# A two-layer decoder trunk on one core: the edges between its stages, its token lists and the order of its attention units

## The reference

```python
def rmsnorm(x, g):
    y = x * lax.rsqrt(jnp.mean(x * x, axis=-1, keepdims=True) + NORM_EPS)
    return y * g

def reference(...):
    h = x
    for layer in range(DEPTH):                       # DEPTH = 2
        xn = rmsnorm(h, norm_mix_g[layer])
        h = h + (rwkv7_time_mix(xn, ...) if layer == 0 else dilated_attention(xn, k_sh, v_sh, w_q, w_o))
        h = h + hier_moe(rmsnorm(h, norm_ffn_g[layer]), ...)
        if layer == 0:
            kv = rmsnorm(h, kv_norm_g) @ w_kv        # keys and values of all three groups
    return rmsnorm(h, final_norm_g)

def dilated_attention(xn, k_sh, v_sh, w_q, w_o):
    q = (xn @ w_q)                                   # 3 groups x 8 heads x 64
    # each group: windowed softmax attention with dilation 1, 4 or 16; also its log denominator
    alpha = softmax(stack(lses), axis=0)             # the groups are weighed by it and added
    return (sum(alpha * outs)) @ w_o

def hier_moe(x, ...):                                # 4 groups x 4 experts, top 1 group, top 2 inside
    for e in range(16):
        y = y + gate[:, e] * ((silu(t @ w_gate[e]) * (t @ w_up[e])) @ w_down[e])
```

## Time and profile before

| | us |
|---|---|
| median of 3 runs | 1559.42 (1558.93 to 1560.63) |
| the profiled execution, its own time | 1562.04 |
| its span, first to last instruction | 1560.3 |
| time mixer (to the first instruction of `moe` in layer 0) | about 521 |
| prologue of the experts, layer 0, to the first expert's product | 521 to 557 |
| experts of layer 0, to the second output of the last | 557 to 848 |
| attention stage | 867 to 1202 |
| experts of layer 1, with prologue | 1203 to 1548 |
| final norm | 1549 to 1560 |

### The profile page before, as it was taken

The page is one execution under the profiler, slowest core; times in us unless marked ns, Lnnn a source line. Parts: engine busy times, 40 slices in busy tenths (PEclk is TensorE's granted clock), DMA queues, the critical chain, the costliest instruction groups (busy, mean ns, idle before and its releaser), DMA issues. The chain is left out here.

```text
span 1560.3 us, 29684 instructions
## 1 busy us (share of the span) xinstructions
PE 1380.5 (88%) x11619; PEld 1077.1 (69%) x11619; DVE 1020.5 (65%) x1346; ACT 846.2 (54%) x1257; POOL 377.5 (24%) x413
## 2 busy tenths in 40 slices
PE   4999996776779899999998599999988899999993
PEld 2276686666664578788786487778767778787872
DVE  5627652445634488999996535675434698998986
ACT  6535552444421358888883334444542488888872
POOL 1112063435450013222223200001120023222322
PEclk9999897999999899999999699999978799999997
DMA  5042300052442579999995332121201799999974
GB/s 170 16 147 81 135 1 15 11 158 86 131 152 101 216 264 383 379 377 378 384 381 192 108 97 82 55 81 55 81 1 46 278 352 386 382 380 379 379 276 163
DMA packets 172042, 301.90 MB, mean 193 GB/s; under 512 B 34573, under 2 KB 44941, under 8 KB 171936
## 3 DMA queue, kind: packets, MB, share of 16 engines
q1 hardware_dynamic: 159648, 271.59, 49.0%
q0 software_dynamic: 11232, 24.61, 4.4%
q10 hardware_dynamic: 1056, 4.19, 0.7%
HBM read 279.96 MB, written 34.60 MB: 202 GB/s over the span
## 5 line engine op out<-in xcount | busy, mean ns | idle before, releaser
L1444 DVE TENSOR_TENSOR moe_wlo<-moe_raw,moe_whi 128x2048 fp32r<-128x2048 f32 x162 | 370.2, 2288 | 35.1 <-ACT moe_whi L1440 30.7
L1440 ACT ACTIVATE moe_whi<-moe_raw 128x2048 fp32r<-128x2048 f32 x192 | 367.0, 1916 | 24.0 <-PE all_bank L1453 22.7
L1451 PE MATMUL all_bank<-moe_whi,moe_xhi 128*128 128x512 f32 x512 | 207.0, 404 | 4.5 <-DVE moe_xlo L1500 4.5
L1452 PE MATMUL all_bank<-moe_wlo,moe_xhi 128*128 128x512 f32 x512 | 199.8, 390 | 0.0
L1453 PE MATMUL all_bank<-moe_whi,moe_xlo 128*128 128x512 f32 x512 | 199.7, 390 | 0.0
L1451 PEld LDWEIGHTS all_bank<-moe_whi,moe_xhi 128*128 128x128 f32 x512 | 96.0, 187 | 27.4 <-DVE moe_xlo L1500 4.4
L1453 PEld LDWEIGHTS all_bank<-moe_whi,moe_xlo 128*128 128x128 f32 x512 | 96.1, 188 | 21.0
L1613 POOL COPY moe_idxcol<-moe_idx 128x1 int32 (+1 forms) x30 | 34.4, 1145 | 312.9 <-PE all_bank L1463 312.9
L1452 PEld LDWEIGHTS all_bank<-moe_wlo,moe_xhi 128*128 128x128 f32 x512 | 96.2, 188 | 18.0
L1451 PE MATMUL all_bank<-moe_whi,moe_hhi 128*128 128x512 f32 x256 | 101.5, 397 | 3.0 <-issue 2.6
L1452 PE MATMUL all_bank<-moe_wlo,moe_hhi 128*128 128x512 f32 x256 | 100.6, 393 | 0.0
(11 more groups left out here) (436 smaller groups left out, 3024.3 us busy)
## 6 DMA issues: line engine op xcount, KB each, us to landing
moe_raw<-in_moe_w_gate_dram SPq DMA_DIRECT2D x64, 1024.0 KB, 9.4
moe_raw<-in_moe_w_up_dram SPq DMA_DIRECT2D x64, 1024.0 KB, 8.8
moe_raw<-in_moe_w_down_dram SPq DMA_DIRECT2D x64, 1024.0 KB, 8.3
attn_xhat<-in_w_kv_dram SPq DMA_DIRECT2D x10, 1024.0 KB, 5.1
out_dram<-all_gain SPq DMA_DIRECT2D x16, 512.0 KB, 4.0
attn_xhat<-in_attn_w_q_dram SPq DMA_DIRECT2D x6, 1024.0 KB, 5.0
all_h<-in_rwkv_w_k_dram SPq DMA_DIRECT2D x4, 1024.0 KB, 8.4
all_h<-in_rwkv_w_v_dram SPq DMA_DIRECT2D x4, 1024.0 KB, 5.0
```

The lines of the kernel that those rows point to most:

```text
L1440: nc.scalar.activation(whi[slot % SPLITS][:, :], raw[slot % 6][:, :], ACT.Copy).then_inc(m["hi_ok"], 1)
L1444: nc.vector.tensor_tensor(wlo[slot % SPLITS][:, :], raw[slot % 6][:, :], whi[slot % SPLITS][:, :].bitcast(fp32), ALU.subtract).then_inc(m[ ...
L1451: nc.tensor.matmul(bank[b][:, :], hi[:, k0 + k, :], wh[:, k, :], start=begin and k == 0, stop=False)
L1452: nc.tensor.matmul(bank[b][:, :], hi[:, k0 + k, :], wl[:, k, :], start=False, stop=False)
```

## The change

The kernel after does five things. (1) `final_norm` goes, and the experts' stage of layer 1 does its work: ScalarE takes the root of a tile right after its squares, VectorE normalises the tiles after the last addition, SyncE sends them out. Both `moe` and `attention` issue one square root on a constant before the squares of h. (2) The attention's first piece comes in two transfers, its split is made two rows of tiles at a time between those of the activations, and TensorE waits for each part of both instead of for all. (3) The token list is made of fp32r products; as an fp32r operand holds fewer bits, the number goes in two parts, 128 j less 512 and the row in the tile, in 32 columns, and VectorE adds the halves. `hot` lies in a weight buffer. (4) `combine` works tile by tile, and the last expert's additions of tile j - 1 follow those of tile j. (5) `beside` begins attention units at two of three steps up to step 35 and again from step 37 on.

```diff
@@ constants
-    for name, n, step, base, per_partition in (("down4", 4, -1, 4, 0), ("base16", 16, P, 0, 0), ("tokless", J, P, -T, 1)):
+    for name, n, step, base, per_partition in (("down4", 4, -1, 4, 0), ("base16", 16, P, 0, 0), ("tokrow", J, P, -T, 0), ("tokpart", 1, 0, 0, 1)):
@@ moe(nc, io, g, layer, result=None)
-        mtok = s.sb("mtok", [P, 2, J, NE])
+        mtok = s.sb("mtok", [P, 2, J, 2 * NE], fp32r)
...
-        hot = yo[:, :].rearrange("p (k j r) -> p k j r", k=2, j=J)
-        late = xn[:, :, :].rearrange("p a b -> p (a b)").rearrange("p (b k j r) -> p b k j r", b=4, k=2, j=J)
+        hot_in = lambda w: w[:, 0:2 * J * P].rearrange("p (k j r) -> p k j r", k=2, j=J)
+        hot, late = hot_in(wlo[3]), [None] + [hot_in(wlo[b]) for b in range(J - 1)]
...
+            if result is not None:
+                for j in range(J):
+                    sp.wait_ge(out_done, j + 1)
+                    sp.dma_start(result[0, P * j:P * j + P, :], h[:, j, :]).then_inc(stored, 16)
+                sp.wait_ge(stored, 16 * J)
...
             for k in range(2):
-                nc.gpsimd.tensor_tensor(mtok[:, k, :, :], ..., g["tokless"]..., ALU.mult).then_inc(mtok_ok, 1)
+                nc.gpsimd.tensor_tensor(mtok[:, k, :, 0:NE], chosen, g["tokrow"]..., ALU.mult).then_inc(mtok_ok, 1)
+                nc.gpsimd.tensor_tensor(mtok[:, k, :, NE:2 * NE], chosen, g["tokpart"]..., ALU.mult).then_inc(mtok_ok, 1)
...
+            nc.scalar.activation(ss[:, 0:1], g["eps"][:, 0:1], ACT.Sqrt).then_inc(root_in, 1)
             for j in range(J):
                 act.wait_ge(last_ok, 2 * j + 2)
                 square_tile(nc, act, g, j, raw[0][:, 0:D], squared)
+                if result is not None:
+                    act.wait_ge(squared, j + 1)
+                    act.wait_ge(root_in, 1)
+                    nc.scalar.activation(ss[:, j:j + 1], g["ss"][:, j:j + 1], ACT.Sqrt, scale=1.0 / D, bias=g["eps"][:, 0:1]).then_inc(rms, 1)
...
-                ch.link(V.tensor_scalar(idxf[:, lo:hi], bank[7][:, lo:hi], float(T), None, ALU.add))
+                ch.link(V.tensor_scalar(by_block(idxf), halves[:, :, 0, :], float(T), None, ALU.add))
+                ch.link(V.tensor_tensor(by_block(idxf), halves[:, :, 1, :], by_block(idxf), ALU.add))
...
-            combine(near, 1, comb_ok)
-            for j in range(J):
-                for half in range(2):
-                    ...
+            for j in range(J):
+                combine(j, near, 1, comb_ok)
+                if j:
+                    add_last(j - 1)
+            add_last(J - 1)
...
+            if result is not None:
+                dve.wait_ge(par_in, PAR + 16)
+                for j in range(J):
+                    dve.wait_ge(rms, j + 2)
+                    V.reciprocal(rstd[:, j:j + 1], ss[:, j:j + 1]).then_inc(rstd_ok, 1)
+                    dve.wait_ge(rstd_ok, j + 2)
+                    V.scalar_tensor_tensor(out=h[:, j, :], in0=h[:, j, :], scalar=rstd[:, j:j + 1], in1=gb[:, :], op0=ALU.mult, op1=ALU.mult).then_inc(out_done, 1)
...
-            pe.wait_ge(mtok_ok, 2)
+            pe.wait_ge(mtok_ok, 4)
             pe.wait_ge(hot_ok, 2)
-            token_list(bank[7][:, 0:NE], hot).then_inc(idx_mm, 1)
+            token_list(bank[7][:, 0:2 * NE], hot).then_inc(idx_mm, 1)
@@ attention
+        def first_hi(act, ks):
+            act.wait_ge(first_in if ks[0] == 0 else piece_in[0], 16)
+            for k in ks:
+                nc.scalar.activation(whi[0][:, k, :], raw_of(0)[:, k, :], ACT.Copy, scale=gain(0, k)).then_inc(hi0_ok, 1)
+
+        def first_lo(dve, ks):
+            for k in ks:
+                dve.wait_ge(hi0_ok, k + 1)
+                nc.vector.scalar_tensor_tensor(out=wlo[0][:, k, :], ...).then_inc(lo0_ok, 1)
...
-            if 0 <= q < 24:
+            if q < 0:
+                return None
+            if q < 24 + 12:
                 return 2 * (q // 3) + q % 3 if q % 3 < 2 else None
-            if 24 <= q < 40:
-                return (q - 24) // 2 + MID if q % 2 else None
-            return q - 40 + FAR_AT if q >= 40 else None
+            return FAR_AT + 2 * ((q - 37) // 3) + (q - 37) % 3 if q >= 37 and (q - 37) % 3 < 2 else None
...
+                if n == 0:
+                    for sem, ks in ((first_in, slice(0, 2)), (piece_in[0], slice(2, 4))):
+                        sp.dma_start(raw_of(0)[:, ks, :], ...).then_inc(sem, 16)
+                    continue
...
-            split_hi(act, 0)
             for kt in range(KT):
+                if kt % 4 == 0:
+                    first_hi(act, range(kt // 2, kt // 2 + 2))
...
+            nc.scalar.activation(ss[:, 0:1], g["eps"][:, 0:1], ACT.Sqrt).then_inc(root_in, 1)
...
-            split_lo(dve, 0)
             for kt in range(KT):
+                if kt % 4 == 0:
+                    first_lo(dve, range(kt // 2, kt // 2 + 2))
...
-                pe.wait_ge(lo_ok, n + 1)
+                if n:
+                    pe.wait_ge(lo_ok, n)
...
-                        elif u == 0:
-                            pe.wait_ge(xl_ok, KT)
+                    if n == 1 and i == 0:
+                        pe.wait_ge(xl_ok, KT)
                     for k in range(4):
+                        if n == 0:
+                            pe.wait_ge(xl_ok, max(i, k) + 1)
+                            pe.wait_ge(lo0_ok, k + 1)
...
-def final_norm(nc, io, g, out):
...
-            moe(nc, io, g, 1)
-            final_norm(nc, io, g, out)
+            moe(nc, io, g, 1, out)
```

More of the change, by code:

```diff
@@ L1326, in _, with moe @@
             product(3)
-def moe(nc, io, g, layer):
+def moe(nc, io, g, layer, result=None):
     h, bank = g["h"], g["bank"]
@@ L1582, in _ @@
                 load_piece(sp, main, n, slot, "down", NE - 1, half)
-            if layer == 1:
+            if result is not None:
                 sp.wait_ge(xn_ok, J)
```

96 lines of the change are left out of this document (46 added, 50 removed).

## The result

The changed kernel takes 1547.12 us (median of 4 runs, 1542.75 to 1548.11) against 1559.18 us for the kernel before on the same chip. The ratio is 0.9915, with a 95% interval of 0.9896 to 0.9933. The kernel became faster, as forecast, but by half as much: 12 us came, 25 were forecast, and 1547 lies outside the range of 1525 to 1542. The profiled execution took 1548.11 us with a span of 1546.3, 14.0 us less than the span before.

A forecast was written before the change was run, and what follows sets the result against it. Where TensorE is busy throughout at clock 1.00 only its work counts; gains lie where it falls short. Six terms sum to 25.0 us: 1562.04 profiled becomes 1537.0, and 1534.4 as the median is 2.6 lower; range 1525 to 1542.

The forecast's parts named there:

- experts' loops: Experts' stages of both layers: order unaltered, a shift of their start moves them whole, so 0 us in the sum.
- token lists: Prologue of both expert layers: one fp32r instruction a product saves eight instructions, net 1.53 us a layer, 3.06 us in all.
- additions mixed: End of the experts, both layers: last-expert additions fill VectorE's waits for returned tiles and close both, 4.13 us.
- table loads: Roots at attention and layer 1's experts: early roots move two ScalarE table loads to where it waits, 2.56 us.
- attention on parts: Edge from experts to attention: TensorE starts on parts of the first piece, 5.6 us gained, bounds 1.1 and 7.9.
- units: Last steps of attention: denser units earlier leave fewer TensorE waits at the end, 6.2 us gained, bounds 0 and 12.4.
- final norm: After layer 1's last addition: early roots leave four reciprocals and products in 5.7 us instead of 9.2, gaining 3.5 us.
- Rival D: Prologue: the one-pass token list takes as long as the fp32 one, giving 1537.9 us; chance 0.05.
- Rival C: Roots: the 1.29 us ahead of each removed table load is a drain that goes too, giving 1530.5 us; chance 0.03.
- Rival A: Last steps of attention: stalls only move to steps 37 to 43, units gain nothing, giving 1540.6 us; chance 0.17.
- B: Tail behind attention: the clock stays high, its 16.2 us shrink by up to 8.1, giving 1526.3 us; chance 0.10.
- E: Attention's slots 6 to 8: VectorE makes TensorE wait, the clock falls to 1.2 GHz, slower, up to 1585 us; chance 0.07.

The follow-up runs named there:

- e1: The changed kernel with its new one-column tile made a fifth column of the token-row tile, so buffers start where they did before: 1539.44 us, ratio 0.9849.
- the aligned kernel: The changed kernel with its new one-column tile put into the token-row tile, restoring the old buffer starts; run twice: 1539.44 and 1533.78 us.
- e9: The aligned kernel run once more, unchanged, as the measure for runs beside it: 1533.78 us, ratio 0.9835.
- e4: The kernel before with only the six buffers that the experts' weights are loaded into moved by 32 bytes: 1571.42 us, ratio 1.0071.
- e7: The aligned kernel with the old token list, sixteen matrix instructions for eight products: 1533.22 us, ratio 0.9829.
- e8: The aligned kernel with all gathered additions ahead of the last expert's additions again: 1540.56 us, ratio 0.9876.
- e2: The kernel before with one unused tile of 32 bytes a partition, so every buffer behind it starts 32 bytes later: 1574.17 us, ratio 1.0082.

## Why the prediction was right in most of its terms and wrong in its sum

The step that failed is the sentence at the end of the first part: "The experts' loops I leave alone: the change does not alter their order, and a shift of their start moves them whole." The order is unchanged, but the loops stood at the rate of their loads, which the page of the profile showed (DMA at 9 of 10 and 377 to 386 GB/s in eleven of its slices) and I did not read, because TensorE had no gap there. So the sum holds 0 for the loops, and none of the five rivals names them. The added tile, which I costed only by its two operations under the first loads, moved the weight buffers off multiples of 256 bytes. The loops became 7.04 and 6.56 us longer, and without the shift they were back at 290.6 and 290.7 us (e1). In both loops of the changed kernel, and in most of those of the aligned one, the first 10 us also ran at a granted clock of 0.83 to 0.85 instead of 1.00, which costs about 1.1 us (290.7 against 289.6 us in the two loops of e9); both loops of the kernel before started at 1.00. That cost, too, was not forecast. The time mixer's 1.4 us more is within its own spread and not shown to belong to the shift.

| term | forecast | measured |
|---|---|---|
| token lists | 3.06 | 0.4 a layer at the high clock, 1.6 at the low: 0.8 to 3.2 |
| additions mixed | 4.13 | 1.8 to 3.0 |
| table loads | 2.56 | 2.56 |
| attention on parts | 5.6 | 6.4 to 7.0 |
| units | 6.2 | 6.6 |
| final norm | 3.5 | 3.6 |
| **sum** | **25.0** | **21.8 to 26.0** |
| experts' loops | 0 | -13.6 |

- **Token lists.** The step of 0.2175 us an instruction (0.21 measured) and 1.53 us a layer (1.0 to 1.8) hold at the low clock. That the level at which the list runs differs from run to run, and 0.4 is all there is at the high one, was missing. The prologues gained 6.5 us in the profiles, more than the list can give: the 32 transposes ahead of it took 6.61 us before and 4.69 and 5.60 after, at a granted clock of 0.55 against 0.78 and 0.65. Runs with the old list (e4, e7) show the fast transposes too, so that part is no effect of the change. Rival D (the one-pass list takes as long as the old one) fell.
- **Additions.** The mechanism holds, the size does not: 1.8 to 3.0 us for 4.13. The forecast summed two waits a layer from one execution and let both close. The waits differ from run to run (e8 has one a layer), and in layer 1 of the changed kernel 0.97 us of one was left.
- **Table loads** as forecast. Rival C fell: the gap ahead of the root is as long without the load as with it.
- **Attention on parts.** The 2.3 us that I added for products at the low level are what was off, and so was the reason, that the level was low at this edge. TensorE, idle for under a microsecond instead of 7, kept the high clock. That gives the upper bound of 7.9 less some waits. The trace of the kernel before could have told it. There too the granted clock had risen to 1.00 by the end of the 32 transposes, as the rows below the list show.
- **Units.** 6.6 against 6.2, and TensorE's waits in the last stretch near the forecast: 4.96 us against 6.1. The wait after the last step, which I had left as it was, shrank from 3.55 to 2.61 us. Rival A (the stalls only move) fell, B too: the tail kept its 16.2 us at 0.50. E fell: TensorE was busy for 47.58 of 48 us at 1.00 in the denser slots.
- **Final norm** as forecast.

TensorE alone at this edge in the kernel before, from its 32 transposes to the first product (us, busy, granted clock, DMA, GB/s):

```profile
870.00:874.00 4.00, 4.00 (x20) 0.50 1.03 401
874.00:875.00 1.00, 1.00 (x10) 0.81 0.06 23
875.00:876.00 1.00, 0.68 (x7) 1.00 0.00 0
876.00:882.50 6.50, 0.00 (x0) 0.64 0.49 161
```

The clock rises while the transposes (`nc.tensor.transpose`) run, and the products behind the idle time start at the low level. The prediction gave that idle time as the reason why no run shows whether transposes count for the clock. The idle time hides nothing: the high level came while TensorE made transposes alone.

Without the shift the forecast is about met: the aligned kernel has ratios of 0.9849 and 0.9835, which on the median of 1559.42 us are 1535.9 and 1533.7 us, against the 1534.4 forecast. By medians, 1539.44 and 1533.78 us, it is 20.6 and 24.5 us faster than the kernel before beside it. That the sum comes so near is luck in part: the start of attention gave 0.8 to 1.4 us more than forecast, the additions 1.1 to 2.3 less. The aligned kernel beats both others; against the changed one, on ratios to the same kernel before, by 0.6 to 0.8%.

What stays open: why a start 128 bytes past the boundary slows a packet less than one of 32 or 64 (it costs 2 to 3 us a loop, they cost 3.4 to 7); why the second loop of the kernel before lost less than the first; and where the rest of the 14 us of e2 lies.

## What to carry to other kernels

A change that adds or resizes any buffer changes where all later ones start; print those starts before and after, and keep the targets of heavy loads at multiples of 256 bytes; here the kernels with such starts were the fast ones, and 32, 64 and 128 bytes past them all cost time. When one engine looks like the only bound of a loop, look at the transfer rate as well: a loop in which both are full has no slack. Here a packet that took 2% longer made the loops 1.2 to 2.4% longer. And read small terms in their own stretch, between instructions that both kernels have, since totals hide 3 us of chance.

## What was not expected of the hardware

- Loads in rows of 2048 bytes into buffers that start 32 or 64 bytes past a multiple of 256 cost the DMA engines 2.1 to 2.2% more time for the same bytes (764.5 against 780.8 to 781.5 us), 128 bytes past it 1.8% (778.3 us; the share is printed to 0.1%, 0.8 us either way). A packet of 2048 bytes took 92.0 to 92.2 ns instead of 89.9 to 90.5, with 128 bytes 91.4. The rate under full load fell from 380 to 366 GB/s, and a piece of 1 MB landed after 12 to 14 us instead of 8 to 10.
- The time mixer, one instruction stream in all these kernels but for its constants, took 519.5 to 527.6 us in the 17 traces; in the 40 slices of the profiles the granted clock in it falls at different moments.
- During 32 transposes of 128 x 128 in fp32 the granted clock rose from 0.50 to 1.00, at the start of attention before and after the change, and TensorE kept it over 0.65 us without work but not over 6.86 us.
